# Time mix of a hybrid decoder step: both held value products ahead of gram block 2, and the five token-major blocks in a row

## The reference

```
def step(S, inp):
    r_t, d_t, k_t, v_t, kk_t, a_t = inp
    Sk = jnp.einsum('bhij,bhj->bhi', S, kk_t)
    S = S * d_t[:, :, None, :] - Sk[..., None] * (kk_t * a_t)[:, :, None, :] + v_t[..., None] * k_t[:, :, None, :]
    return S, jnp.einsum('bhij,bhj->bhi', S, r_t)
```

## Time and profile before

| | |
|---|---|
| median of 3 runs | 1483.69 us (1480.75 to 1483.72) |
| the profiled execution | 1484.89 us |
| its span | 1483.2 us, 36430 instructions |
| TensorE, loads, VectorE, ScalarE, GpSimd busy | 98%, 73%, 58%, 38%, 25% |
| granted clock of TensorE, mean | 0.996 of full |
| data moved | 165.38 MB, mean 112 GB/s |

### The profile page before, as it was taken

The page is one execution under the profiler, slowest core; times in us unless marked ns, Lnnn a source line. Parts: engine busy times, 40 slices in busy tenths (PEclk is TensorE's granted clock), DMA queues, the critical chain, the costliest instruction groups (busy, mean ns, idle before and its releaser), DMA issues.

```text
span 1483.2 us, 36430 instructions
## 1 busy us (share of the span) xinstructions
PE 1455.8 (98%) x14550; PEld 1079.1 (73%) x14550; DVE 856.4 (58%) x1712; ACT 556.2 (38%) x1356; POOL 370.9 (25%) x483
## 2 busy tenths in 40 slices
PE   6999999999999999999999999999999999999998
PEld 4555577777888888777777777777777777777753
DVE  3153556668777777456667686767676522023533
ACT  3156555542222222246364635454545232210000
POOL 0000141220111211125131322212131046355452
PEclk9999999999999999999999999999999999999999
DMA  9913688833566665411121212121112225342311
GB/s 322 324 57 103 178 255 275 260 93 111 128 156 159 155 162 139 118 45 33 39 55 44 55 33 53 34 52 41 45 40 59 55 81 174 86 150 77 121 43 50
DMA packets 191537, 165.38 MB, mean 112 GB/s; under 512 B 38559, under 2 KB 169631, under 8 KB 190344
## 3 DMA queue, kind: packets, MB, share of 16 engines
q1 hardware_dynamic: 182359, 128.17, 31.1%
q0 software_dynamic: 8352, 32.52, 7.3%
q10 hardware_dynamic: 656, 2.36, 0.5%
HBM read 136.93 MB, written 26.08 MB: 110 GB/s over the span
## 4 chain that ended last, share of the span: by engine, by line
PE 88%; DVE 6%; DVEq 2%; ACT 1%; issue 1%; DMA 1%; POOL 0%; POOLq 0%; SPq 0%
PE me_bank L3270 13%; PE rw_bank L1912 11%; PE sa_psOs L1245 8%; PE sa_psS L1198 7%; PE pr_psZ L751 4%; PE me_bank L3308 3%; PE fr_bankL L317 3%; PE fr_bankL L251 2%; PE pr_psS L739 2%; PE rw_bank L1948 2%; DVE rw_gram L2772 2%; PE sa_psT L1208 2%; PE rw_bank L1924 2%; PE pr_psT L762 1%; PE pr_psO L774 1%; PE sa_psS L1187 1%
## 5 line engine op out<-in xcount | busy, mean ns | idle before, releaser
L1912 PE MATMUL rw_bank<-hT,big 128*128 128x288 f32 x336 | 94.1, 419 | 0.1
L1306 ACT COPY kpe<-sa_psS 128x512 f32<-128x512 f32 x64 | 34.4, 589 | 134.5 <-PE sa_psS L1198 134.5
L1035 POOL DMA_DIRECT2D big<-in_cache_kv x68 | 37.6, 552 | 147.0 <-issue 146.8
L751 PE MATMUL pr_psZ<-hT,qlT 128*128 128x288 f32 x256 | 73.9, 408 | 0.0
L1912 PEld LDWEIGHTS rw_bank<-hT,big 128*128 128x128 f32 x336 | 59.7, 189 | 16.0 <-ACT big L2423 1.7
L3346 ACT COPY big<-me_bank 128x288 f32<-128x288 f32 x42 | 16.7, 398 | 144.8 <-PE me_bank L3270 144.8
L1035 POOL DMA_DIRECT2D pages<-in_cache_kv x68 | 37.5, 552 | 118.0 <-issue 118.0
L751 PEld LDWEIGHTS pr_psZ<-hT,qlT 128*128 128x128 f32 x256 | 46.6, 189 | 20.1 <-issue 8.4
L1245 PE MATMUL sa_psOs<-big,sa_ST 128*128 128x257 f32 x256 | 60.3, 386 | 0.0
L1245 PE MATMUL sa_psOs<-pages,sa_ST 128*128 128x257 f32 x256 | 60.3, 385 | 0.0
L1402 DVE TENSOR_TENSOR sa_ST<-sa_psT,kinvp 128x512 f32<-128x512 f32 x64 | 42.9, 678 | 27.8 <-PE sa_psT L1208 27.7
(11 more groups left out here) (653 smaller groups left out, 3718.9 us busy)
## 6 DMA issues: line engine op xcount, KB each, us to landing
big<-in_w_in SPq DMA_DIRECT2D x44, 512.0 KB, 4.0
big<-in_cache_kv POOLq DMA_DIRECT2D x68, 128.0 KB, 3.8
pages<-in_cache_kv POOLq DMA_DIRECT2D x68, 128.0 KB, 3.2
fr_wada<-in_w_ada SPq DMA_DIRECT2D x8, 1024.0 KB, 11.8
big<-in_cache_kv SPq DMA_DIRECT2D x60, 128.0 KB, 2.9
pages<-in_cache_kv SPq DMA_DIRECT2D x60, 128.0 KB, 3.2
qk_scratch<-oaT SPq DMA_DIRECT2D x32, 192.0 KB, 2.6
fr_wada<-in_w_ada SPq DMA_DIRECT2D x2, 2048.0 KB, 12.4
```

The source lines that it names most:

```text
L751: last = nc.tensor.matmul(psZ[h][:, 0:HT], M.wz[hp % 2][:, k, :], M.hT[:, k, h * HT:(h + 1) * HT], start=(k == 0), stop=(k == KT - 1))
L1035: e.dma_start(M.pages[s % 2][q * QP:(q + 1) * QP, g, :, 0:KL], src).then_inc(landed, 16)
L1306: nc.scalar.copy(S.rearrange("q (c p j) -> q p c j", c=2 * GP, p=GP)[:, :, cs, :], got[:, :, cs, :]).then_inc(copied, 1)
L1912: last = mm(into, held, moving, start=(k == 0 and n in (1, 2, 7)), stop=(k == K4 - 1), skip_group_check=True)
```

## The change

Only TensorE's order at the head of each turn changes; no instruction is added or taken away. In turns 1 to 7 product 4 comes directly behind product 7, ahead of gram blocks 2 and 3, where it stood behind block 3. In turn 0 `values_up` moves in the same way. Block 4 now comes directly behind block 3, ahead of the transposes of block 0, and the five `token_major` blocks follow each other (with the bonus sums ahead of the fourth in turn 0, as before).

```diff
--- before.py
+++ after.py
@@ -2213,21 +2213,18 @@
                 grams(i, 1)
                 if i:
                     multiply(i, VZ, 7)
+                    multiply(i, VZ, 4)
                     pe.wait_ge(o_sb, i)
                 else:
+                    tail.values_up()
                     pe.wait_ge(px_sb, 6)
                 grams(i, 2)
                 pe.wait_ge(gram_sb, NU * i + 2)
                 grams(i, 3)
-                if i:
-                    multiply(i, VZ, 4)
-                else:
-                    tail.values_up()
-                pe.wait_ge(mixed, 3 * i + 3)
-                token_major(i, 0)
                 pe.wait_ge(gram_sb, NU * i + 4)
                 grams(i, 4)
-                for c in range(1, C5):
+                pe.wait_ge(mixed, 3 * i + 3)
+                for c in range(C5):
                     if i == 0 and c == 3:
                         bonus_sums(0)
                     token_major(i, c)
```

## The result

The changed kernel takes 1503.27 us (median of 4 runs, 1501.06 to 1503.43), the kernel before 1482.22 (4 runs beside it, 1480.52 to 1483.72): 1.0134 times as long, 95% interval 1.0116 to 1.0151, 21 us more. The profiled execution took 1503.43 us.

The account below looks back on a forecast made before the run. VectorE's queue order was taken to bound the stage. Seven turns at 3.0 us (21.0) plus 1.3 for turn 0 gave 22.3 us on the median of 1483.69, so 1506.0; range 1499 to 1520.

Parts of the forecast that it names:

- from the add's end to product 4: Turns 1 to 7: TensorE starts product 4 0.05 us after VectorE's value add ends, as after other releasing instructions.
- product 4: Turns 1 to 7, TensorE: it lasts as long as product 7, which has its shape, 2.14 us.
- block 2's start to copy 4: Block 2 needs 1.28 us from its first matmul to VectorE's first copy of it.
- copies 4 and 5 late, a turn: VectorE, turns 1 to 7: these copies start 3.0 us late in each turn; seven turns make 21.0 us (15.4 to 22.4).
- turn 0: Value output of the samples moves ahead of block 2; VectorE is late by 1.3 us (0 to 2).
- What bounds the stage: VectorE's queue order sets the stage's end; block 2 reaches it just in time, 805.85 beside 805.78, with no cushion.
- Nothing takes it up: Behind the stage TensorE, ScalarE and GpSimd all wait for this level's results, so the 3.0 us a turn remain.
- The clock: Rival: longer TensorE idles halve the clock in some turns too; three drops make 1515 us, seven 1527; chance 0.22.
- The idle times of the changed stage: TensorE idles 1.5 us between transposes 1 and 2 and 0.7 us around the inverse level in each turn.
- Absorption: Rival: bank found free or a later wait hides part; 16.7 us in all, 1500.4, down to 1490; chance 0.10.
- lower bound: If product 4 didn't wait for the value add, block 2's copies would come 2.2 us late in each turn.
- TensorE ends the stage: Rival: only TensorE's order counts, so the change saves 5.6 us in 8 turns, 1478.1; chance 0.03.

Follow-up runs that it names:

- the row of five alone: Kernel before, with only block 4 moved ahead of the transposes of block 0, so five token-major blocks follow each other; 1484.63 us, ratio 1.0018.
- the wait alone: Kernel before, nothing moved; TensorE only waits for the first value add ahead of gram block 2 in turns 1 to 7; 1489.65 us, ratio 1.0051.
- half a product: Kernel before, with two of product 4's four weights moved ahead of gram block 2 in turns 1 to 7; 1498.03 us, ratio 1.0101.
- product 4 alone: Kernel before, with only product 4 moved ahead of gram block 2 in turns 1 to 7; 1504.04 us, ratio 1.0143.
- the value output alone: Kernel before, with only the value output of the samples moved ahead of block 2 in turn 0; 1482.86 us, ratio 0.9998.
- product 4 behind block 2: Changed kernel, but product 4 (in turn 0 the value output of the samples) stands between blocks 2 and 3; 1485.87 us, ratio 1.0016.
- without the wait: Changed kernel, but product 4 goes into bank 0 as its own sum and needn't wait for the first value add; 1494.20 us, ratio 1.0084.

## Why the prediction was right

The forecast was 1506.0 for the median, 22.3 us more; measured were 1503.3 and 21.0, with an interval of 17.2 to 22.4 us. The terms of the sum, each measured by itself (those of turns 1 to 7 in turn 2):

| term | predicted | measured |
|---|---|---|
| from the add's end to product 4 | 0.05 us | 0.10 |
| product 4 | 2.14 | 2.11 |
| block 2's start to copy 4 | 1.28 | 1.18 |
| copies 4 and 5 late, a turn | 3.0 | 2.9 |
| turn 0 | 1.3 | 1.4 |
| sum (seven turns of 2.9, by the stages, and turn 0) | 22.3 | 21.7 |

- *What bounds the stage.* VectorE's queue without a gap and block 2 just in time: the row of five alone, the wait alone and half a product bear this out. Each delay of block 2 came out at the last transpose almost in full (the table under half of product 4), and TensorE's order behind it made no difference. The step that was most off is the 1.28 us from block to copy. It was read at block 0 of turn 0, and in the changed kernel block 0 has 1.28 us there again (661.32 to 662.60), but block 2 has 1.18, in turn 0 (665.31 to 666.49) as in turn 2. Why the first block takes 0.1 us longer is open. The break ahead of product 4 was short by 0.05 us, so that the two errors partly cancel.
- *Turn 0.* VectorE's rows have the predicted delay:

```profile
662.60 2.64 DVE L2769 COPY_PREDICATED rw_gram<-see,rw_bank 128x512 f32<-128x512 int32 x4 [2.78 <-PE rw_bank L1977]
666.49 1.33 DVE L2769 COPY_PREDICATED rw_gram<-see,rw_bank 128x512 f32<-128x512 int32 x2 [1.25 <-PE rw_bank L1977]
...
675.27 0.24 DVE L2674 STREAM_TRANSPOSE rw_XT<-rw_X 64x64 f32<-64x64 f32 x1
```

The wait for block 2 is 1.25 us where 1.3 was forecast, and the stage is 1.4 us longer.
- *Nothing takes it up.* The rest of turns 2 to 6 is 56.33 us for 56.49, so this held.
- *The clock.* The forecast left the clock as it was, with a rival by which it falls in some of the turns 1 to 7, and such a dip was named as a sign of being wrong. The sign came, once: in the profile after, the drop of turn 0 is gone and a shorter one stands in turn 1 (rows as in the earlier trace rows):

```profile
704.00:710.00 6.00, 5.96 (x73) 5.21 (x72) 2.02 (x5) 5.91 (x10) 0.00 (x0) 1.00 0.54 131
747.00:748.00 1.00, 0.90 (x30) 0.65 (x16) 0.85 (x4) 0.37 (x1) 1.00 (x1) 0.77 0.00 0
748.00:750.00 2.00, 2.00 (x77) 1.33 (x74) 1.83 (x5) 1.26 (x3) 2.00 (x4) 0.50 0.03 8
750.00:751.00 1.00, 1.00 (x3) 0.71 (x4) 1.00 (x2) 0.92 (x4) 1.00 (x2) 0.53 0.21 60
```

The rest of turn 1 takes 57.38 us with it, for 56.20 before, so it cost 1.2 us. Of the nine profiles this is the only one with a dip in turns 1 to 7, so it is not shown that the longer idle times bring one about; and on the whole the clock was no lower. The price put on turn 0's drop, 3.0 us, was right: the rest of turn 0 takes 57.32 us with it and 54.23 without. The mean clock was 0.9975 of full in the 36 executions of the kernel before that ran beside the experiments and 0.9988 with the changed one (4). 0.001 is 1.6 us here, by a line through those 36 (1478.29 and 1480.56 at 1.000, 1484.47 to 1487.02 at 0.996). Brought to one clock by that line, the mean of the changed kernel is 21.7 us above the kernel before; from the executions at 0.999 alone it is 23.2 (1503.26, median of 3, to 1480.05, median of 7). The line is good to some 2 us only: for product 4 alone it makes 18.4 us of means 21.0 apart, where the stages give 20.3. So it is the stage times that bear the sum out; that the medians came out at 21.0 rather than 21.7 is within their interval, and the clock's share in it was not forecast.
- *The idle times of the changed stage.* The 1.5 us between transposes and 0.7 us around the level, which the prediction gave without a working, are 1.28 and 0.59 us in turn 2.
- *The other rivals.* Absorption didn't happen at this place. Without its wait the product would have cost 1.9 us a turn and not the 2.2 of the lower bound. That bound had counted a second 2.14 us, which is product 7 with a break; two products in one stream take 2.05 and 2.03 us. That TensorE ends the stage is excluded by the row of five.

## What to carry to other kernels

Where two engines hand work to each other in a fixed order, the place of an independent piece of work is judged by the consumer's queue: put it ahead of something that the consumer takes later, with room to spare, not ahead of what it takes next. The same 2.1 us of matmuls cost 2.9 us ahead of block 2 and 0.23 us behind it, though the product itself is needed by nobody in between. A piece that waits for the other engine brings that wait (0.8 us here) with its first instruction. And a kernel whose busiest engine is shown 98% busy can still be bound, stage by stage, by the order of another.

## What the hardware showed that was not expected

The granted clock falls to half in single stretches of some 3.4 or 6.8 us, in some executions and not in others, and with it goes most of the scatter of this kernel: 0.995 to 1.000 on the mean, 1478 to 1487 us in the 36 executions, of whose variance the line takes three quarters.

- In turn 0 it stood at 0.50 through 704 to 710 us in three profiles (before, product 4 alone, the wait alone), those in which this turn began at 661.6 to 661.8 us. In those that began it at 659.2, 660.6, 661.3, 663.2 (two) and 664.2 us it held there, or fell for half as long (half of product 4).
- It also falls outside the time mix. In the row of five alone and the value output alone it was at 0.50 for nearly 7 us at 609 to 616 us, and for half as long in half of product 4; these are the three profiles in which turn 0 began latest. Six of the nine have a further stretch between 21 and 28 us. The profile of product 4 behind block 2 has neither, nor one in the time mix; its turn 0 began first and its mean clock is 1.000. So the moment at which turn 0 begins goes with the drops ahead of it.

The kernels with the value output of the samples ahead of block 2 (changed, turn 0 alone, without the wait; 20 runs) had a mean clock of 0.9987, the six that leave it behind block 2 (72 runs) means of 0.996 to 0.9975. Whether it is the order of turn 0 or its moment that keeps the clock up was not tried apart and stays open; the order of turn 0 can't act on the stretches ahead of it.
